# A hybrid attention and short-convolution layer on eight cores: new stage order, scale folded into the key/value weights, own tokens in quarters, half of the output projection inside the attention

## The reference

```python
shift, scale, gate = split(silu(c) @ w_mod + b_mod)          # each (B, 2048)
h_ctx = rms_norm(ctx, norm_g) * (1 + scale_c) + shift_c      # 256 context tokens
h     = rms_norm(x,   norm_g) * (1 + scale) + shift          # 4096 latent tokens
q, k, v, ga, b, cg, hh, gc = split(h @ w_in)                 # 1024,256,256,1024, 4 x 1024 columns
q, k = rms_norm per head of 128, times q_g / k_g; 2-D rotary on latent q, k
o    = softmax(q [k_ctx; k]^T / sqrt(128)) [v_ctx; v]        # 8 heads, 2 kv heads, 4352 keys
attn = silu(ga) * o
conv = silu(gc) * (b * conv3(cg * hh))                       # depthwise, width 3 over tokens
x    = x + gate * (concat(attn, conv) @ w_out)
out  = rms_norm(x, final_norm_g)
```

## Time and profile before

| what | value |
|---|---|
| median of 3 runs | 1186.58 us (1186.1 to 1188.34) |
| the profiled execution: its own time | 1188.4 us |
| its span, first to last instruction, slowest core (core 3) | 1186.7 us |
| spans of the eight cores | 1171.2 to 1186.7 us |
| granted PE clock, mean | 0.967 on core 3 |
| busy: PE, ACT, DVE, POOL | 962.8, 505.3, 428.9, 149.1 us |
| chain that ended last, shares | PE 68%, DMA 17%, DVE 6%, ACT 4%, issue 3% |
| HBM read | 171 MB |

### The profile page before, as it was taken

One profiled execution on the slowest core, in us unless ns is written; L12 is line 12 of the kernel. 1 busy time (PEld: TensorE's weight loads), 2 busy tenths in 40 slices (PEclk: granted clock), 3 DMA queues, 4 the chain that ended last, 5 costly groups with the idle time before them and its releaser, 6 DMA issues.

```text
span 1186.7 us, 16921 instructions; the slowest of 8 cores (1171.2 to 1186.7 us)
## 1 busy us (share of the span) xinstructions
PE 962.8 (81%) x5604; PEld 457.5 (39%) x5604; DVE 428.9 (36%) x782; ACT 505.3 (43%) x902; POOL 149.1 (13%) x180
## 2 busy tenths in 40 slices
PE   0111269778899999999999989898989899889995
PEld 0111135344444444444444443333434344334442
DVE  0000134724756820222222223344444444424554
ACT  0000346443544421000000019899999899932111
POOL 0000002344234510011111000000000000000000
PEclk9999979898899999999999999899999999989998
DMA  9999984455449216666666307700000000022442
GB/s 143 177 161 171 171 218 87 85 183 98 81 80 160 46 36 107 107 107 107 107 107 110 69 1 142 142 1 1 1 1 1 1 1 1 1 107 75 165 170 89
DMA packets 20389, 107.30 MB, mean 90 GB/s; under 512 B 2256, under 2 KB 12880, under 8 KB 12880
## 3 DMA queue, kind: packets, MB, share of 16 engines
q0 software_dynamic: 5760, 73.44, 36.0%
q1 hardware_dynamic: 14544, 32.78, 8.0%
HBM read 171.26 MB, written 8.39 MB: 151 GB/s over the span
## 4 chain that ended last, share of the span: by engine, by line
PE 68%; DMA 17%; DVE 6%; ACT 4%; issue 3%; SPq 0%; DVEq 0%; ACTq 0%; POOLq 0%; POOL 0%
PE PS L824 19%; PE PS L982 10%; PE PS L943 8%; PE PS L897 8%; DMA R<-w_mod 5%; PE PS L921 5%; PE PS L795 5%; DMA big<-xT 4%; PE PS L479 4%; DMA R<-w_out 4%; PE PS L713 4%; DMA ident_f<-ident 3%; PE PS L471 2%; DMA R<-w_in 2%; DVE big L415 1%
## 5 line engine op out<-in xcount | busy, mean ns | idle before, releaser
L933 ACT ACTIVATE work<-PS,smx 128x1024 bf16<-128x1024 f32 x272 | 291.1, 1113 | 18.3 <-DVE work L948 8.0
L824 PE MATMUL PS<-R 128*128 128x512 bf16 x1024 | 228.6, 378 | 0.0
L948 DVE TENSOR_TENSOR work<-work 128x512 bf16<-128x512 bf16 x272 | 127.8, 471 | 170.9 <-ACT work L933 112.8
L943 PE MATMUL PS<-work,V 128*128 128x512 bf16 x544 | 164.4, 384 | 8.8 <-DVE work L908 4.4
L897 PE MATMUL PS<-big,KT 128*128 128x512 bf16 x544 | 164.4, 384 | 0.2 <-ACT work L844 0.2
L824 PEld LDWEIGHTS PS<-R 128*128 128x128 bf16 x1024 | 97.9, 97 | 117.7
L921 PE MATMUL PS<-work,ones_bf 128*128 128x512 bf16 x272 | 104.3, 383 | 26.2 <-DVE work L948 26.0
L982 PE MATMUL PS<-R,big 128*128 128x512 bf16 x512 | 113.0, 384 | 3.9 <-POOL big L913 3.9
L357 PE MATMUL PS<-s_bf,R 128*128 128x2 bf16 x512 | 14.6, 165 | 107.0 <-DMA R<-w_mod 69.6
L479 PE MATMUL PS<-R,big 128*128 128x512 bf16 x384 | 93.5, 400 | 0.0
L839 DVE TENSOR_TENSOR work<-PS,work 128x512 f32<-128x512 f32 x16 | 11.1, 691 | 201.4 <-PE PS L824 176.3
(11 more groups left out here) (118 smaller groups left out, 946.2 us busy)
## 6 DMA issues: line engine op xcount, KB each, us to landing
R<-w_mod POOLq DMA_DIRECT2D x8, 2048.0 KB, 22.4
R<-w_conv POOLq DMA_DIRECT2D x8, 2048.0 KB, 16.7
big<-xT POOLq DMA_DIRECT2D x6, 2048.0 KB, 18.7
big<-xT SPq DMA_DIRECT2D x2, 4096.0 KB, 22.6
wg<-w_gate POOLq DMA_DIRECT2D x8, 1024.0 KB, 19.0
R<-w_out POOLq DMA_DIRECT2D x4, 2048.0 KB, 14.2
big<-xown SPq DMA_DIRECT2D x8, 1024.0 KB, 4.9
out<-big SPq DMA_DIRECT2D x8, 1024.0 KB, 4.2
```

Of the source, the lines that this page charges most:

```text
L824: P.op("tensor", lambda e, wb4=wb4, kc=kc, g=g, tt=tt, b=b: e.matmul(bank(b), wb4[:, kc, g, :], hT_own[:, kc, tt * 512:(tt + 1) * 512], st ...
L933: P.op("scalar", lambda e, sp=sp, pp=pp: e.activation(out=PT[pp], in_=PS[sp][:], func=AF.Exp, scale=sm_scale, bias=smx[:, 2:3]), reads=[ps ...
L943: P.op("tensor", lambda e, ob=ob, chunk=chunk, g=g, pp=pp, cl=cl: e.matmul(bank(ob), V[:, chunk, g * 128:(g + 1) * 128], PT[pp][:, cl * 51 ...
L948: P.op("vector", lambda e, pp=pp, tq=tq: e.tensor_tensor(out=tmpb[tq], in0=PT[pp][:, 0:512], in1=PT[pp][:, 512:1024], op=ALU.add), reads=[ ...
```

## The change

The program is written anew; `Prog` now derives its waits from the bytes that an operation touches, and buffers are laid out by hand in nine 16 KB slots. What it does in another way:

- **Modulation order.** The four scale tiles of w_mod are loaded first, then the key/value weights, then x tiles. After each scale tile its quarter of `gm` is formed and folded into the weights `wkv2` on DVE. The four shift tiles are loaded and multiplied between the key/value tiles.
- **Other tiles** (`kv_other`, six of 512 tokens): 64 gram matmuls, one DVE multiply and one reduction for the four diagonals, 64 matmuls of 512 columns; keys are kept raw in float32 (`kraw`), values scaled straight into `V`. No bias here: the values' bias is added after the attention (`bv`), the keys' later.
- **Context and own tokens** follow the fourth and fifth tile: the context, then four quarters of 256 tokens, through two float32 buffers `x32` that SP fills, with the multiply by the row norm split between DVE (9 chunks) and POOL (7), and the fronts between DVE (10) and ACT (6).
- **Keys' norm and rotary**: squares on POOL beside the query stage (`k_stage1`), rotary and transposes beside the attention gate (`k_stage2`, `k_put`), for eight tiles of 512 tokens.
- **Queries**: qg is folded into the cosine and sine tables; the rotary runs on DVE for three blocks of four, on POOL for one; `qT` is copied by ACT.
- **Output gate**: by 16 matmuls of 256 columns per group with the condition spread over 128 columns (`sbc`), straight into `gate_bc`.
- **Attention**: two pairs of score banks in place of three, the output alternates between banks 4 and 5, the sums lag by two to four steps, the norm is two ACT and two DVE operations with none on POOL; all w_out loads go to buffers that the convolution has left. Heads of the first 512 tokens come first. From the ninth pass on each step also does 2 of the 256 matmuls of output blocks 0 to 3, in bank 7.
- **Output**: evacuation by 512 columns on DVE alone (multiply, add, multiply with sum), halves of 1024 scaled and written; x blocks are loaded by SP from the ninth pass on.

```diff
+    load("wst0", wst[0], dr["w_mod"][4])
+    load("wst1", wst[1], dr["w_mod"][5])
+    load("wkv", wkv, dr["w_in"][2])
+    load("xb0", xb[0], dr["xT"][0])
+    for t in range(4):
+        c = 4 * t
+        mod_tile(t, 16 + c, 5 + t % 2)
+        P.stt(gm[:, c:c + 4, :], m_sb[:, 16 + c:20 + c, :], 1.0,
+              ng_sb[:, c:c + 4].unsqueeze(2).broadcast_to([128, 4, 2]), ALU.add, ALU.mult)
+        for kc in range(c, c + 4):
+            P.ts(V_, wkv2[:, kc, :], wkv[:, kc, :], gm[:, kc, 0:1], ALU.mult)
+        if t < 2:
+            load(f"wst{t}", wst[t], dr["w_mod"][6 + t])
+        if t == 1:
+            load("xb1", xb[1], dr["xT"][1])
+        elif t == 2:
+            load("wst0", wst[0], dr["w_mod"][0])
+            load("xb2", xb[2], dr["xT"][2])
+        elif t == 3:
+            load("wst1", wst[1], dr["w_mod"][1])
+    def kv_other(t, beside={}):
+        x = xb[t % 3]
+        gb = 3 + t % 2
+        for blk in range(4):
+            xs = slice(blk * 128, blk * 128 + 128)
+            for kc in range(KC):
+                P.mm(bank(gb)[:, xs], x[:, kc, xs], x[:, kc, xs], kc == 0, kc == KC - 1, kc == KC - 1 and blk == 3)
...
+        for blk in range(4):
+            b = kv_bank()
+            for kc in range(KC):
+                P.mm(bank(b), x[:, kc, blk * 128:blk * 128 + 128], wkv2[:, kc, :], kc == 0, kc == KC - 1, kc == KC - 1)
+            P.ts(V_, kraw[t][:, :, blk, :], bank(b, 256).rearrange("p (h d) -> p h d", h=2), r[:, blk:blk + 1], ALU.mult)
+            P.act(V[:, 2 + t * 4 + blk, :], bank(b)[:, 256:512], AF.Copy, scale=r[:, blk:blk + 1])
+            if blk in beside:
+                beside[blk]()
+    kv_other(0)
+    load("xb0", xb[0], dr["xT"][3])
+    kv_other(1)
+    mod_tile(0, 0, 5)
+    load("wst0", wst[0], dr["w_mod"][2])
+    kv_other(2)
+    mod_tile(1, 4, 6)
+    load("wst1", wst[1], dr["w_mod"][3])
+    load("xb1", xb[1], dr["xT"][4])
+    load("xb2", xb[2], dr["xT"][5])
+    kv_other(3)
+    mod_tile(0, 8, 5)
+    P.dma("sync", "x320", x32[0][:], k3(dr["ctxT"], 256))
+    mod_tile(1, 12, 6)
+    P.dma("sync", "x321", x32[1][:], k3(dr["xq"][0], 256))
+    def own_a(i):
+        P.act(hq(i), x32[i % 2][:], AF.Square)
+    def own_b(i):
+        rstd_mm(hq(i), 6 + i % 2)
+    def own_c(i):
+        x, h, r, row = x32[i % 2][:], hq(i), rstd_bc[i % 2][:], 1 if i == 0 else 0
+        rstd_fin(r, 6 + i % 2)
+        ks = 9
+        bc = r.unsqueeze(1)
+        P.tt(G_, x[:, ks:, :], x[:, ks:, :], bc.broadcast_to([128, KC - ks, 256]), ALU.mult)
+        P.tt(V_, x[:, 0:ks, :], x[:, 0:ks, :], bc.broadcast_to([128, ks, 256]), ALU.mult)
+        for kc in range(KC):
+            if kc % 5 in (1, 3):
+                P.act(h[:, kc, :], x[:, kc, :], AF.Identity, scale=gm[:, kc, row:row + 1],
+                      bias=m_sb[:, kc, row:row + 1])
+            else:
+                P.ts(V_, h[:, kc, :], x[:, kc, :], gm[:, kc, row:row + 1], ALU.mult, m_sb[:, kc, row:row + 1], ALU.add)
+        if i + 1 < 4:
+            P.dma("sync", f"x32{i % 2}", x32[i % 2][:], k3(dr["xq"][i + 1], 256))
...
+    def kv_own(h, blk, kn, kb, chunk):
+        b = kv_bank()
+        for kc in range(KC):
+            P.mm(bank(b), h[:, kc, blk * 128:blk * 128 + 128], wkv[:, kc, :], kc == 0, kc == KC - 1, kc == KC - 1)
+        P.act(kn[:, :, kb, :], bank(b, 256).rearrange("p (h d) -> p h d", h=2), AF.Copy)
+        P.tt(V_, V[:, chunk, :], bank(b)[:, 256:512], bias_sb[:, 256:512], ALU.subtract)
+    kv_other(4)
+    own_a(0)
+    own_b(0)
+    own_c(0)
+    own_a(1)
+    kv_other(5, {0: lambda: own_b(1), 1: lambda: own_c(1)})
+    load("wq0", wq[0], dr["w_in"][0])
+    load("wq1", wq[1], dr["w_in"][1])
+    own_a(2)
+    kv_ctx()
+    own_b(2)
+    own_c(2)
+    own_a(3)
+    halo()
+    kv_quarter(1)
+    own_b(3)
+    k_put(rotk[0], 2, 0, 5)
+    own_c(3)
+    own_a(4)
+    P.dma("sync", "tabq", cosq[:], dr["tab"][6:8, :, 0:512].rearrange("t p (b d) -> p t b d", b=4), group=True)
+    P.dma("sync", "tabq", sinq[:], dr["tab"][6:8, :, 512:1024].rearrange("t p (b d) -> p t b d", b=4), group=True)
+    P.settle("tabq")
+    kv_quarter(2)
+    own_b(4)
+    own_c(4)
+    load("wga0", wga[0], dr["w_in"][3])
+    kv_quarter(3)
+    kv_quarter(4)
...
+        eng = G_ if i % 4 == 1 else V_
+    for i in range(16):
+        q_step(i)
+        if i % 2 == 0:
+            k_stage1(i // 2)
+        if i == 7:
+            load("wga1", wga[1], dr["w_in"][4])
+    for i in range(16):
+        ga_step(i // 2, i % 2)
+        if i < 2:
+            flush(1 - i)
+        if i % 2:
+            t = i // 2
+            k_stage2(t, G_ if t % 2 else V_)
+            if t + 2 < 8:
+                tab_load(t + 2)
+            if t > 0:
+                k_put(rotk[(t - 1) % 2], 4, CTX + (t - 1) * 512, 7)
+        if i == 7:
+            load("wcv1", wcv[1], dr["w_conv"][1].rearrange("p (k g n) -> p k g n", g=4, n=128))
...
+            gate_mm = i - 1
+            for kc in range(KC):
+                P.mm(bank(7, 256), sbc[:, kc, :], wgt[:, kc, :], kc == 0, kc == KC - 1, kc == KC - 1)
+            gs = gate_bc[:, gate_mm * 256:gate_mm * 256 + 256]
+            P.tt(V_, gs, bank(7, 256), gs, ALU.add)
+            load("wgt", wgt, dr["w_gate"][i])
+    sm_scale = 1.0 / math.sqrt(128.0)
+    iters = [(tt, g * 4 + q) for tt in range(2) for g in range(2) for q in range(4)]
+    steps = [(it, p) for it in range(16) for p in range(NP)]
+    def emit_s(i):
+        it, p = steps[i]
+        tt, h = iters[it]
+        for c in range(2):
+            ch = 2 * p + c
+            P.mm(bank((i % 2) * 2 + c), KT[:, h // 4, ch * 128:ch * 128 + 128], qT[tt][:, h, :], True, True, c == 1)
+    def emit_exp(i):
+        P.act(PT[i % 3][:], bank2((i % 2) * 2), AF.Exp, scale=sm_scale, bias=smx[:, 2:3])
+        P.tt(V_, tmpb[i % 6][:], PT[i % 3][:, 0:512], PT[i % 3][:, 512:1024], ALU.add)
...
+    def emit_ones(i):
+        it, p = steps[i]
+        P.mm(bank(6), ones_bf[:], tmpb[i % 6][:], p == 0, p == NP - 1, True)
+    def emit_norm(it):
+        tt, h = iters[it]
+        P.act(lns[:], bank(6), AF.Ln)
+        P.act(rs_sb[:], lns[:], AF.Exp, scale=-1.0)
+        P.tt(V_, ot[:], bank(4 + it % 2), rs_sb[:], ALU.mult)
+        P.stt(mixA[:, h, tt * 512:tt * 512 + 512], ot[:], bv[:, h // 4, 0:1], sga[tt][:, h, :], ALU.add, ALU.mult)
...
+    def y_evac(blk, c, b):
+        x = xo[xbuf(blk)]
+        cs = slice(c * 512, c * 512 + 512)
+        P.tt(V_, ytmp[:], bank(b), gate_bc[:, cs], ALU.mult)
+        P.tt(V_, x[:, cs], x[:, cs], ytmp[:], ALU.add)
+        P.stt(ytmp[:], x[:, cs], 1.0, x[:, cs], ALU.mult, ALU.mult, accum=ss4[blk % 2][:, c:c + 1])
+    def y_end(blk):
+        x = xo[xbuf(blk)]
+        r = rso[blk % 2]
+        P.rsum(r[:], ss4[blk % 2][:])
+        P.act(r[:], r[:], AF.Ln, scale=1.0 / D, bias=eps_sb[:, 0:1])
+        P.act(r[:], r[:], AF.Exp, scale=-0.5)
+        for hf in range(2):
+            cs = slice(hf * 1024, hf * 1024 + 1024)
+            P.stt(x[:, cs], x[:, cs], r[:, 0:1], fg_sb[:, cs], ALU.mult, ALU.mult)
+            P.dma("sync", f"out{xbuf(blk)}{hf}", out[blk * 128:blk * 128 + 128, cs], x[:, cs])
...
+    kcs = list(range(8, 16)) + list(range(8))
+    fill = [(blk, c, j) for blk in range(4) for c in range(4) for j in range(8)]
+    emit_s(0)
+    for i in range(len(steps)):
+        it, p = steps[i]
+        if i + 1 < len(steps):
+            emit_s(i + 1)
+        emit_exp(i)
+        if i > 0:
+            emit_pv(i - 1)
+        if p < 2 and it > 0:
+            emit_ones(i - 2)
+            if p == 1:
+                emit_norm(it - 1)
+        elif p == 4:
+            emit_ones(i - 4)
+            emit_ones(i - 3)
+        elif p == 5:
+            emit_ones(i - 3)
+        elif p == 6:
+            emit_ones(i - 3)
+            emit_ones(i - 2)
+        elif p > 6:
+            emit_ones(i - 2)
+        if it == 8 and p == 3:
+            x_load(0)
+            x_load(1)
+        if (it, p) >= (8, 3) and fill:
+            blk, c, j = fill.pop(0)
+            for kc in kcs[2 * j:2 * j + 2]:
+                y_mm(blk, c, kc, 7)
+            if j == 7:
+                y_evac(blk, c, 7)
+                if c == 3:
+                    y_end(blk)
+                    x_load(blk + 2)
+    assert not fill
+    n = len(steps)
+    emit_pv(n - 1)
+    emit_ones(n - 2)
+    emit_ones(n - 1)
+    x_load(6)
+    for c in range(4):
+        for kc in kcs[:-1]:
+            y_mm(4, c, kc, c)
+        if c == 0:
+            emit_norm(15)
+            x_load(7)
+    for c in range(4):
+        y_mm(4, c, kcs[-1], c)
+        y_evac(4, c, c)
+    y_end(4)
+    for blk in range(5, 8):
+        for c in range(4):
+            b = (4 + c) if blk % 2 else c
+            for kc in kcs:
+                y_mm(blk, c, kc, b)
+            y_evac(blk, c, b)
+        y_end(blk)
```

1445 lines of the change are left out of this document (539 added, 906 removed).

## The result

The change made the kernel **slower**: 1226.84 us in the median of four runs (1211.89 to 1251.49) against 1186.34, and in the two highest the cores of one die ran at a lower clock, so all ratios here are of the other runs: 1.0203, 95% interval [1.0181, 1.0225]. I had forecast 1115 with a range of 1088 to 1150.

A forecast was written before the change was run, and what follows sets the result against it. Transfers limit until 132.4 us, PE with holes from 171.6, PE without holes from 418 to 709, then ACT and PE nearly level. Terms -57.4, -0.6, +4.1, +8.9, -23.4, -3.7 sum to -72.1: about 1115 us, range 1088 to 1150.

The forecast's parts named there:

- Up to the first tile: Start of kernel: six 4 MB tiles at 12.5 us each land first, so PE starts key/value tiles at 82 us.
- The six tiles: Key/value tiles: pace follows transfers, 25 us a pair, 2.6 us restart per wait; fifth at 190 to 210, last ends 238.
- the rival built on it: Key/value tiles: PE cold throughout, 36.6 us each, ending at 302 instead of 238, +64, total 1179; chance 0.03.
- Context and quarters: Before the queries: steps of Square, sums, multiply, fronts overlap with keys; queries start at 298 instead of 355.4, -57.4 us.
- rival 1: Context and quarters: chain exposed each time or loads delayed by POOL's queue; queries start 315 to 332, total 1130 to 1150; chance 0.16.
- Queries: Query stage: PE's work unchanged, DVE, POOL and PE all level, so 62 us instead of 62.6, -0.6.
- Attention gate: Gate stage: 56 transposes add 3.1 us and the odd tile's rotary 1 to 56.8 us, +4.1.
- Convolution: Convolution: matmuls unchanged, gate costs 1.73 instead of 0.78 us a time, plus last transposes 0.5; +8.9 us.
- Tail: After the last matmul: DVE operations, sum, Ln, Exp, two halves and a write take 9.5 us instead of 13.2, -3.7.
- Attention: Attention and projection: cheaper norms and output matmuls as fill give 438.4 us instead of 461.8, -23.4.
- rival 2: Attention: fill replaces norm holes by holes at evacuation, block end and score hand-over, 462 as now, total 1139; chance 0.12.
- the rival for "slower": Attention: two score pairs delay hand-over, 1.7 us for 1.08 on 272 steps, up to +130, total over 1189; chance 0.05.

The follow-up runs named there:

- e3: Changed kernel with the two query weight loads on POOL asked for after the quarters' loads: 1211.56 us, ratio 1.0177 to the kernel before.
- e17: e15 with POOL's part of the reciprocal-norm multiply in context and quarters given to DVE: 1155.08 us, ratio 0.9712.
- e7: Changed kernel with the own key's POOL square, DVE reduction and ACT logarithm spread over three query blocks: 1189.99 us, ratio 0.9991.
- e9: Changed kernel with the first convolution weight's load on POOL issued after the gate stage's table loads: 1224.71 us, ratio 1.0276.
- e12: e9 with the first gate weight asked for ahead of the third convolution weight: 1211.72 us, ratio 1.0172.
- e15: e7 plus constants first, query weights after quarters (second behind sine table), halo earlier, attention norm's end two steps later, query rotaries on DVE: 1162.63 us, ratio 0.9759.
- e18: e17 with no POOL arithmetic before the convolution; key bias and rotaries on DVE, key squares and sums on ACT: 1152.31 us, ratio 0.9698.

## Why the prediction was wrong

**Up to the first tile, 82 for 100.7: wrong step, small consequence.** I counted tiles and never the constants on SP, though the kernel before had its identity matrix in after 31.2 us only. The fifth tile at 198.4 lies within 190 to 210, but in part by luck: tiles 2 to 4 came 19 us apart, at PE's pace and not 25 behind transfers, since the late start had let their transfers run ahead, and then PE waited 8.5 us for the fifth. An error of size lies inside: I priced a 2 MB load through SP by its bytes in memory at half a tile, 6.25 us. It takes 10.6 alone (e3), and the kernel before already had twice its size at 22.6:

```profile
big<-xT SPq DMA_DIRECT2D x2, 4096.0 KB, 22.6
```

**The six tiles: the clock right, the end 16.6 us late.** The clock is 0.92 in their stretch, and the slow part is short, as the earlier trace rows had it: the first tile's 64 gram matmuls took 5.9 us and the fifth's 6.5, the others' 3.7. The Trainium skill's rule on loops that wait for transfers (TensorE: Matmul & The Clock Gate, "Loop structure matters more than you think") costs here a few us, not 64; the trace does not bear out the rival built on it. But the sixth tile ends at 254.6 for 238. I let ACT's Square of the context run beside the fifth tile; it stands on ACT behind the tile's last copy of V and starts at 219.8, PE waits 4.8 us for it, and 4.9 for the first quarter's where I had 3.

**Context and quarters, 298 for 331.3: rival 1's number.** The halo's sums start at 288.6 for 259. Quarter 3: "at 240 and meets the two 4 MB query tiles on POOL, so it lands near 253": it left SP at 259.5 and took 25 us for 13. "POOL multiplies ... beside DVE's 9/16": not beside, but behind. "12 us idle" at the halo's sums: 22.4. And rival 1 was given 0.16. The runs give 4.6 us for the order of the loads, 7.1 for the halo's place, 6.5 for POOL's part of the multiply, and 14.6 for all of these at once (e17); the rest of the 33 stays without an experiment.

**Queries, -0.6 for +27.8: the step that failed worst.** "All level, so 62 us" adds up each engine's work and takes the largest sum, with DVE, POOL and PE in parallel. The runs show that the order of the instructions costs 20 of the 28 us. For the other 8, DVE held beside POOL is the likely cause, not a shown one: it is held some 20 us in e7's stage, but each kernel that took work off POOL there stayed at 70 or more. The rows of before could have warned: the earlier trace rows has the rotary's multiply of 512 at 1.04 us where the earlier trace rows also has 0.69 for a multiply of the same size, and I wrote the 1.04 into the sum without asking what it was.

**Attention gate, +4.1 for +22.1.** Of the 18 over the forecast, 7.7 us are a leftover of the late query transposes at its start (gone in e7), 6.0 the table's load (gone in e9 and e12) and some 4 the half speed behind these two waits. With POOL's arithmetic gone the stage took 68.6.

**Convolution: right**, 244.0 for 245.8. **Tail: wrong**, 13.7 for 9.5: my sum began with DVE free at the last matmul, and it was 4.7 us behind.

**Attention, -23.4 for -8.9: mechanism right, a term missing.** Waits of PE on ACT in the second half: 19.1, where I had 6.3 + 1.7 + 11.6 = 19.6. What I left out is the slow restart behind the waits, some 7 us, though I had priced it at 2.6 us for the key/value tiles, and one wait of 2.6 us for the first evacuation on DVE. With the norm late the attention takes 435.6 for 438.4 in e15: rival 2 (nothing given back) is out.

The side of zero was missed because the rival for "slower" looked only at the attention; the queries' order was nowhere a rival, though the change puts the key's chain over three engines between its blocks.

## What to carry to other kernels

When a stage is costed by the largest of its engines' sums, write its instructions down per queue for two rounds and follow one value through: a short instruction that waits (a logarithm of eight numbers) holds all that its engine has queued behind it. Work on POOL beside DVE is not free and often not even a gain: where both read two inputs from SBUF, price the two as one engine (DVE's multiplies of 512 out of PSUM stayed at 0.69 us throughout). And give each load on SP, small or large, the time of at least one of the tiles in flight on POOL on top of its own, once for each load that stands in SP's queue: move the tile, and look again at what then stands behind it. To judge an edit ahead of a stage, measure from a point behind which only the edit differs, not from the start of the kernel.

## What the runs showed of the hardware

- Small loads on SP came in one for each tile of POOL while such tiles were in flight, some 12 us apart: the ninth was in at 94.7 us, behind two tiles at 34.2, behind none at 8.3. A 2 MB load landed between two tiles of POOL, after 25 us for 10.6 alone. What holds them no run shows. The Trainium skill (DMA: Bandwidth & Descriptors, "Queues, rings and completion order") says that a DMA engine goes round its queues packet by packet; by that a small load should have been in early. The measurement differs, and it decides.
- In e18 PE's matmuls took 0.27 us each instead of 0.2159 for nearly 100 us on core 3, busy and hardly waiting, at a granted clock of 0.81, between the two levels of the other rows (1.00, and half of it behind a wait). Core 4, on the other die, had 1.00 from 292 to 326 us. Windows and PE timeline of core 3:

```profile
310.00:326.00 16.00, 16.00 (x62) 6.63 (x61) 9.49 (x15) 8.30 (x43) 0.00 (x0) 0.81 1.03 171
```

```profile
326.54 4.37 PE L173 MATMUL PS<-wq,hT 128*128 128x512 bf16 x16
```

What sets it no run here shows. Core 4's query stage took 77.8 us, like core 3's 77.7, so in e18 the clock alone does not explain this stage's length.
